# A hybrid layer's start: three blank products, and the first loads in smaller pieces and another order

## The reference

```python
def memory_cross_attention(q, mem, w_mem_kv):
    kv = mem @ w_mem_kv                                   # mem 256 x 1024, w_mem_kv 1024 x 1024
    k = kv[..., :512].reshape(b, m, 4, 128)               # the memory's keys, 4 heads
    v = kv[..., 512:].reshape(b, m, 4, 128)               # the memory's values
...
def hybrid_layer(x, mem, w_in, ...):
    proj = x @ w_in                                       # x 2048 x 1024, w_in 1024 x 9216
    (q_sb, k_sb, v_sb, g_sb, u_pool, g_pool, u_lru, g_lru, q_xa, g_xa, merge) = _split_columns(proj)
...
    y_xa = memory_cross_attention(q_xa, mem, w_mem_kv) * silu(g_xa)
...
    log_a = (-8.0 * r) * softplus(-lru_L)                 # the recurrence's decay rates
...
    return layer_norm(2 ** 0.25 * x + merged @ w_out, ln_g, ln_b)
```

## Time and the profile before

| | us |
|---|---|
| runs of the kernel | 2309.51, 2309.39 and 7796.06; median 2309.51 |
| profiled execution, its own time | 2309.13 |
| span of the profiled execution | 2307.2 |
| what lies around the span (2309.13 - 2307.2) | 1.93 |
| TensorE busy | 2294.4 (99%) |
| TensorE's weight loads busy | 1901.3 (82%) |
| VectorE, GpSimd, ScalarE busy | 1411.6 (61%), 1217.3 (53%), 1059.9 (46%) |

### The profile page before, as it was taken

How to read it: one execution, slowest core, us unless ns; L and a number is a source line. 1 busy time by engine, 2 the same in 40 slices (tenths; PEclk the granted TensorE clock), 3 DMA queues, 4 the chain that set the end, 5 groups by cost and what they waited for, 6 DMA issues and landing times. The chain is left out here.

```text
span 2307.2 us, 30158 instructions
## 1 busy us (share of the span) xinstructions
PE 2294.4 (99%) x10952; PEld 1901.3 (82%) x10952; DVE 1411.6 (61%) x1658; ACT 1059.9 (46%) x1643; POOL 1217.3 (53%) x847
## 2 busy tenths in 40 slices
PE   9999999999999999999999999999999999999998
PEld 6888888888878888888888888888888778888887
DVE  7555552763487465468887777723844695465476
ACT  5555542442484245332576676632342683355220
POOL 1666653864456354435476566644763565345341
PEclk9999999999999999999999999999999999999999
DMA  6544422124343312273344544322133334312442
GB/s 233 189 157 158 147 71 96 55 83 137 104 112 124 132 51 79 100 280 140 109 156 142 164 152 137 110 96 73 56 126 130 85 106 145 102 55 87 145 166 82
DMA packets 102898, 281.06 MB, mean 122 GB/s; under 512 B 9952, under 2 KB 31584, under 8 KB 101728
## 3 DMA queue, kind: packets, MB, share of 16 engines
q1 hardware_dynamic: 101024, 273.90, 36.1%
q10 hardware_dynamic: 1728, 5.24, 0.7%
HBM read 207.80 MB, written 62.91 MB: 117 GB/s over the span
## 5 line engine op out<-in xcount | busy, mean ns | idle before, releaser
L2287 POOL TENSOR_TENSOR WLS<-SR,WHS 128x512 fp32r<-128x512 f32 x264 | 408.1, 1564 | 121.7 <-ACT WHS L1115 110.9
L772 PE MATMUL J<-XBH,WHS 128*128 128x512 f32 x1152 | 453.1, 393 | 0.0
L774 PE MATMUL J<-XBH,WLS 128*128 128x512 f32 x1152 | 449.3, 390 | 0.0
L773 PE MATMUL J<-XBL,WHS 128*128 128x512 f32 x1152 | 448.9, 390 | 0.0
L772 PE MATMUL J<-XBH,WH 128*128 128x512 f32 x864 | 340.0, 394 | 0.2
L774 PE MATMUL J<-XBH,WL 128*128 128x512 f32 x864 | 337.1, 390 | 0.0
L773 PE MATMUL J<-XBL,WH 128*128 128x512 f32 x864 | 336.7, 390 | 0.0
L774 PEld LDWEIGHTS J<-XBH,WLS 128*128 128x128 f32 x1152 | 216.3, 188 | 46.0
L773 PEld LDWEIGHTS J<-XBL,WHS 128*128 128x128 f32 x1152 | 216.5, 188 | 43.3 <-issue 0.2
L772 PEld LDWEIGHTS J<-XBH,WHS 128*128 128x128 f32 x1152 | 216.4, 188 | 43.2 <-DVE XBL L1668 0.2
L1701 DVE TENSOR_TENSOR ST<-J,ST 128x512 f32<-128x512 f32 x160 | 109.5, 685 | 228.1 <-PE J L774 182.1
(11 more groups left out here) (302 smaller groups left out, 4756.4 us busy)
## 6 DMA issues: line engine op xcount, KB each, us to landing
RAW<-w SPq DMA_DIRECT2D x144, 512.0 KB, 3.7
pk_m<-MB SPq DMA_DIRECT2D x56, 512.0 KB, 5.0
MB<-pk_m SPq DMA_DIRECT2D x48, 512.0 KB, 4.1
KC<-pk_k SPq DMA_DIRECT2D x40, 512.0 KB, 5.3
VC<-pk_v SPq DMA_DIRECT2D x40, 512.0 KB, 4.4
BRAW<-w SPq DMA_DIRECT2D x64, 256.0 KB, 5.2
XRAW<-xt SPq DMA_DIRECT2D x8, 1024.0 KB, 12.6
pk_v<-STL SPq DMA_DIRECT2D x16, 512.0 KB, 5.1
```

Of the source, the lines that this page charges most:

```text
L772: nc.tensor.matmul(to, wh, xh, start=first, stop=True, skip_group_check=True)
L773: nc.tensor.matmul(to, wh, xl, start=False, stop=True, skip_group_check=True)
L774: return nc.tensor.matmul(to, wl, xh, start=False, stop=True, skip_group_check=True)
L2287: low = G_.tensor_tensor(WLS[:, k, :], SR[:, k, :], WHS[:, k, :].bitcast(F32), ALU.subtract)
```

## The change

A buffer BLANK (128 x 384) is filled by VectorE, and TensorE makes three products of it into J0, which nobody reads. The first quarter of MRAW is loaded as two blocks, and MW tile 0 as a quarter, a quarter and a half; TensorE waits for each by itself. The value tiles come as quarters, quarters and halves, and stand ahead of x blocks 1, 2 and 3. Four value products stand ahead of piece 1 (two for each of the two groups of memory rows), 12 ahead of piece 4. On ScalarE the cast of x block 1 comes behind `keys_of(2)` and `keys_of(3)`, and the rates' exponential goes to piece 6 of pair 1. On VectorE `x_sum(0, T1 + 1)` and `unit_lo(0, 1)` change places, and the two operations on the rates move behind the rests of the memory's values (piece 9 of pair 0). Declarations of semaphores are left out:

```diff
+        BLANK = at("BLANK", R, [P + MEM])
...
-            for i in range(4):
+            sp.dma_start(MRAW[:, 0:1], memt[:, 0:1]).then_inc(m_first, 16)
+            sp.dma_start(MRAW[:, 1:2], memt[:, 1:2]).then_inc(m_in[0], 16)
+
+            for i in range(1, 4):
                 load_memory(i)
             load_mw(1)
             load_w(0, 0)
             load_w(0, 1)
             load_mw(2)
             load_mw(3)
-            for j in range(2):
-                load_x(0, j)
-            for part, made in enumerate((mv_first, mv_second)):
-                s = slice(part * KD // 2, (part + 1) * KD // 2)
+
+            def load_values(ks, made):
                 for k in range(HEADS, MEM_TILES):
-                    sp.dma_start(MW[:, k, s].rearrange("p k n -> p (k n)"), w8[k, :, part * D // 2:(part + 1) * D // 2]
+                    sp.dma_start(MW[:, k, ks].rearrange("p k n -> p (k n)"), w8[k, :, ks.start * P:ks.stop * P]
                                  ).then_inc(made, 16)
-                load_x(0, 2 + part)
+
+            load_x(0, 0)
+            load_values(slice(0, 2), mv_first)
+            load_x(0, 1)
+            load_values(slice(2, 4), mv_second)
+            load_x(0, 2)
+            load_values(slice(4, 8), mv_third)
+            load_x(0, 3)
...
+            pe.wait_ge(blank, 1)
+            for _ in range(3):
+                nc.tensor.matmul(J[0][:, 0:MEM], BLANK[:, 0:P], BLANK[:, P:], start=True, stop=True)
             for h in range(HEADS):
                 pe.wait_ge(big_raw[h] if h else mw_first, 16)
                 for k in range(KD):
-                    if h == 0 and k % 2 == 0:
+                    if h == 0 and k < 2:
+                        pe.wait_ge(m_in[0] if k else m_first, 16)
+                    elif h == 0 and k % 2 == 0:
                         pe.wait_ge(m_in[k // 2], 16)
+                    if h == 0 and k == 2:
+                        pe.wait_ge(mw_second, 16)
                     if h == 0 and k == KD // 2:
                         pe.wait_ge(big_raw[0], 16)
...
-                    if m == 0 and k in (0, KD // 2):
-                        pe.wait_ge(mv_second if k else mv_first, 16 * HEADS)
+                    if m == 0 and k in (0, 2, 4):
+                        pe.wait_ge((mv_first, mv_second, mv_third)[k // 2], 16 * HEADS)
...
-                pair(g0, {} if half else {2: lambda: memory_all_values(0, range(2)),
-                                          4: lambda: (memory_all_values(0, range(2, KD)), memory_all_values(1, range(KD)),
+                pair(g0, {} if half else {1: lambda: (memory_all_values(0, range(2)), memory_all_values(1, range(2))),
+                                          4: lambda: (memory_all_values(0, range(2, KD)), memory_all_values(1, range(2, KD)),
                                                       pe.wait_ge(c_made, CONSTANTS))})
...
-            for part, made in enumerate((mw_first, big_raw[0])):
-                s = slice(part * KD // 2, (part + 1) * KD // 2)
-                act.dma_start(MW[:, 0, s].rearrange("p k n -> p (k n)"), w8[0, :, part * D // 2:(part + 1) * D // 2]
+            for ks, made in ((slice(0, 2), mw_first), (slice(2, 4), mw_second), (slice(4, 8), big_raw[0])):
+                act.dma_start(MW[:, 0, ks].rearrange("p k n -> p (k n)"), w8[0, :, ks.start * P:ks.stop * P]
                               ).then_inc(made, 16)
             keys_of(0)
             first_tile(0)
             keys_of(1)
             sums_of(0, False)
             unit_hi(0, 0)
-            unit_hi(0, 1)
             keys_of(2)
             keys_of(3)
+            unit_hi(0, 1)
...
-                    pair(g0, {3: lambda: (values_out(), [unit_hi(half, u) for u in (8, 9, 12, 13)]),
-                              13: exponential_of_rates})
-                pair(g0 + 1, {5: lambda: deviation(half - 1, TB - 1), 8: lambda: load_queries(half, 0)} if half else {7: lambda: load_queries(half, 0)})
+                    pair(g0, {3: lambda: (values_out(), [unit_hi(half, u) for u in (8, 9, 12, 13)])})
+                pair(g0 + 1, {5: lambda: deviation(half - 1, TB - 1), 8: lambda: load_queries(half, 0)} if half else
+                     {6: exponential_of_rates, 7: lambda: load_queries(half, 0)})
...
+            V_.memset(BLANK[:], 1.0).then_inc(blank, 1)
             keys_rest(0)
...
             x_sum(0, T1)
+            x_sum(0, T1 + 1)
             unit_lo(0, 1)
-            x_sum(0, T1 + 1)
...
-            dve.wait_ge(c_in, 32)
-            link(V_.tensor_scalar(SM[:, KB:2 * KB], L, -1.0, None, ALU.mult))
-            link(V_.tensor_tensor(SM[:, 0:KB], SM[:, KB:2 * KB], L, ALU.max))
+
+            def rates():
+                dve.wait_ge(c_in, 32)
+                link(V_.tensor_scalar(SM[:, KB:2 * KB], L, -1.0, None, ALU.mult))
+                link(V_.tensor_tensor(SM[:, 0:KB], SM[:, KB:2 * KB], L, ALU.max))
...
-                              5: lambda: [unit_lo(0, u) for u in (11, 12, 13)], 9: memory_values_rest})
+                              5: lambda: [unit_lo(0, u) for u in (11, 12, 13)], 9: lambda: (memory_values_rest(), rates())})
```

More of the change, by code:

```diff
@@ L315, in build @@
         c_in, c_made, exp_l, small = sem("c_in"), sem("c_made"), sem("exp_l"), sem("small")
-        m_in, mw_first = [sem(f"m_in{i}") for i in range(4)], sem("mw_first")
-        mv_first, mv_second = sem("mv_first"), sem("mv_second")
+        blank = sem("blank")
+        m_in, m_first, mw_first, mw_second = [sem(f"m_in{i}") for i in range(4)], sem("m_first"), sem("mw_first"), sem("mw_second")
+        mv_first, mv_second, mv_third = sem("mv_first"), sem("mv_second"), sem("mv_third")
         mk_hi, mk_kept = sem("mk_hi"), sem("mk_kept")
```

## The result

The changed kernel takes 2312.51 us (median of 22 runs, 2311.36 to 2314.27), the kernel before 2309.45: **3.06 us slower**, ratio 1.0014 with a 95% interval of 1.0008 to 1.002. The forecast was 2309.1, and no end of its range reaches the result. The profiled execution took 2312.49 us.

What follows compares the result with a forecast made beforehand. TensorE bounds the kernel (2294.4 of 2307.2 us busy), VectorE and GpSimd set pair 1's start; +0.45 - 0.60 = -0.15 us gave 2309.0 or 2309.4 from two baselines, forecast 2309.1, range 2308.1 to 2309.9.

Steps and rivals of the forecast that it cites:

- The first loads: Smaller first pieces of MRAW and MW: first product at 4.1 instead of 4.66 us, later blocks landing as before.
- The slower rival: Second x block becomes the bound through slow quarters or a late GpSimd sum: 2309.6 to 2310.4 us, chance 0.17.
- the prediction's two signs of being wrong: TensorE runs into pair 1 without waiting, or waits at the third key tile much longer than 12.7 us.
- The places that it named: Doubled weight-load pace before 9 us, first x product near 19.7, second x cast near 20.5, pair 1's WL ending near 53.5.
- The rates: Two small operations leave VectorE's chain before pair 1's WL: -0.40 us, hidded there by ScalarE's casts; afterwards in spare time.
- The blank product: At the start, filled by 1.4 us, costs nothing up to 0.1 us, lets the clock rise from 1.4 instead of 4.66.
- The first key product: TensorE's first product at the start, taken at 4.1 us, between 4.66 (no gain) and some 3.9 (half the bytes).
- The quarters: Value loads ahead of x block 1 delay it by 1.5 us, adding 0.45 us to VectorE's chain.
- the 3.8 us: Time for the four value quarters at the DMA page's 138 GB/s, instead of 1.5; the sum some 2 us higher.
- block 1's delay: Second x block's later landing puts +0.45 us on VectorE's chain toward pair 1's WL.
- forecast 0.60 less: Before pair 1's WL, GpSimd's earlier sum runs beside VectorE's add and covers its step: -0.60 us.
- The caution: At ScalarE's last key cast: TensorE over 0.6 us later than 20.5 would delay the second x cast one for one.

## Why the prediction was wrong

**The first loads, the step that failed.** The prediction said that "the bytes ahead of every later load are the same, so the later blocks land when they landed before". The bytes are the same, but the engines fell out of step, and x block 0 was complete at 18.66 instead of 16.45. Cost: 2.3 us alone, 2.5 us in the changed kernel, where the prediction had only a gain. The prediction priced small loads only at the value quarters, behind a full queue, where they were harmless. The page DMA: Bandwidth & Descriptors, Bandwidth, of the Trainium skill, which I weighed there (batch the transfers), had its place at the first loads: 242 to 292 GB/s where 346 to 375 had been. The same page, Two DMAs through the same engine are not ordered, says that nothing orders transfers across the 16 engines; the landings 2.5 us apart agree. The slower rival named a late second x block, but gave the value quarters or a late GpSimd sum as its cause and stopped at 2310.4. Neither of the prediction's two signs of being wrong appeared: TensorE did wait at pair 1, and it came to the third key tile at 15.04, behind the tile's landing at 14.88. The places that it named told more: the doubled pace before 9 us, 19.7, 20.5 and 53.5 became 10.94, 21.98, 22.73 and 55.85.

**The rates, the second that failed.** "Behind WL the two operations run in VectorE's spare time": they had none there, and the second one took 1.14 us beside GpSimd's sum. Cost 0.46 us in the trace; the times say the same within their scatter (+0.61 alone, from +0.58 to -0.32 when moved on), and neither is clear. The Trainium skill's page SBUF — State Buffer, Who interferes with whom, says that a VectorE instruction with two SBUF inputs contends with a GpSimd instruction that reads SBUF; the 1.14 us beside the sum agree. I had read that taking of turns off the three XBL subtractions, and did not ask it of a 128 x 4 operation.

**What held, and what held by luck.** The blank product was filled in 0.38 us (bounds 0 to 0.68). The first key product's 4.04 against 4.1 is luck: its loads landed by 3.61, ahead of the lower bound (half the bytes give 4.66 - 0.64 = 4.02, not 3.9), and the blank products, priced at nothing, held it to 4.04. The quarters put 4.04 us between the x blocks instead of 2.5 (forecast 1.5 us more: 22.70 - 18.66 = 4.04); the 3.8 us that the prediction set beside that did not come. With the first loads back, TensorE came at 19.56 (19.7), and WL of pair 1 ended at 51.50 + 1.92 = 53.42, 0.2 earlier (0.15): block 1's delay was made up, as forecast, where the three XBL subtractions beside GpSimd took 5.12 us instead of 5.67 (forecast 0.60 less). The caution that TensorE's lateness would delay the second cast one for one came true in the run with the values back. With both faults mended the time was 2309.45, against 2309.1 forecast and 2309.77 of the kernel before in that set; 0.32 us is no clear gain.

**Where the blank products' gain went.** As forecast, WL of pair 1 takes some of it: with four 0.46 of the 1.08, after the wait at 21.36 had taken 0.31. That it comes at all seems to hang on the gap behind the last blank product, or on a wait soon after, which the prediction had not seen: in the changed kernel TensorE stood for 1.40 us after two key products, and the pace doubled at 10.94, later than before.

**Still open:** by what the first small loads bring the engines out of step, and why a long load ahead kept them together in one trace and not in the other. SyncE's slow issue of the RAW loads goes with it (1.27 to 2.19 us in the five traces where the first loads of both queues are small, 0.92 to 1.11 in the eight where they are as before); no run tells whether it is the cause or follows.

## What to carry to other kernels

Price a smaller first load not by its bytes but by the last of the 16 engines to land, and look at the landings of the loads far behind it: here 0.6 us earlier at the front cost 2.2 us on everything after. A tiny operation costs what its engine waits for, so ask of a new place which other engine runs beside it and not only whether there is room. Look at what a warm-up leads into: here it brought TensorE 1.1 us forward with gaps up to 0.26 us ahead of the real work and nothing with 0.77, the next waits took most of that, and no run was clearly faster.

## What had not been expected of the hardware

Loads of 128 KB as the first of two queues left the 16 DMA engines 2.5 us apart (2.22 to 2.73 in five traces) for the next 20 us and more, with packets of 1 KB and of 2 KB alike; as later loads they left 0.55 to 0.64. A subtraction-sized wait (1.14 us) came upon an operation on 128 x 4 elements. TensorE's pace doubled at 4.5 to 4.9 us when four or five blank products ran up to the first key product, at 5.8 and 7.2 when 0.23 and 0.26 us lay between, and at 8.6 and 9.3 with 0.52 and 0.77.
